# Output projections of both layers from seven half-size products, PSUM banks of the first pinned, one embedding product moved ahead of the turned rows

## Time and profile before

| | |
|---|---|
| median of 3 runs | 1343.76 us (1342.78 to 1344.82) |
| the profiled execution's own time | 1345.24 us |
| its span, first to last instruction | 1343.3 us |
| TensorE busy (matmul) | 1058.4 us, 79% |
| VectorE / ScalarE / GpSimd busy | 412.1 / 179.7 / 90.7 us |
| mean granted TensorE clock | 0.918 of full speed |
| moved by DMA | 474.88 MB, mean 354 GB/s |

### The profile page before, as it was taken

How to read it: one execution, slowest core, us unless ns; L and a number is a source line. 1 busy time by engine, 2 the same in 40 slices (tenths; PEclk the granted TensorE clock), 3 DMA queues, 4 the chain that set the end, 5 groups by cost and what they waited for, 6 DMA issues and landing times.

```text
span 1343.3 us, 26339 instructions
## 1 busy us (share of the span) xinstructions
PE 1058.4 (79%) x10962; PEld 628.8 (47%) x10962; DVE 412.1 (31%) x884; ACT 179.7 (13%) x429; POOL 90.7 (7%) x227
## 2 busy tenths in 40 slices
PE   6999988666677667679999999988666765776578
PEld 5885444333344334344688554445333433433343
DVE  1694323112112111226674544432111111121116
ACT  2344311000000000011121000221000000000001
POOL 0100011000000000000110100011000000000000
PEclk9999999888888888899999999999888888888889
DMA  9846799999999999999454236699999999999992
GB/s 360 322 162 245 293 406 427 428 428 428 428 428 428 429 429 429 428 414 367 153 188 148 103 126 239 279 395 426 428 428 429 429 428 428 428 427 429 429 421 100
DMA packets 57841, 474.88 MB, mean 354 GB/s; under 512 B 4057, under 2 KB 6105, under 8 KB 32193
## 3 DMA queue, kind: packets, MB, share of 16 engines
q1 hardware_dynamic: 56800, 470.32, 84.9%
q10 hardware_dynamic: 768, 2.57, 0.5%
q0 software_dynamic: 224, 1.31, 0.3%
HBM read 473.12 MB, written 3.16 MB: 355 GB/s over the span
## 4 chain that ended last, share of the span: by engine, by line
DMA 49%; PE 45%; DVE 2%; issue 2%; ACT 1%; SPq 1%; POOL 0%; DVEq 0%; ACTq 0%; POOLq 0%
DMA big<-in_moe_w_up_dram 48%; PE ps L920 10%; PE ps L663 7%; PE ps L1105 5%; PE ps L686 4%; PE ps L1019 3%; PE ps L654 3%; PE ps L733 2%; PE ps L644 2%; PE ps L1167 2%; PE ps L942 1%; PE ps L831 1%; PE ps L950 1%; SPq L527 1%; PE ps L848 1%
## 5 line engine op out<-in xcount | busy, mean ns | idle before, releaser
L920 PE MATMUL ps<-big 128*32 128x256 f32 x4064 | 322.6, 485 | 161.2 <-DMA big<-in_moe_w_up_dram 161.0
L920 PEld LDWEIGHTS ps<-big 128*32 128x32 f32 x4064 | 166.1, 138 | 312.5 <-issue 179.7
L1741 DVE SCALAR_TENSOR_TENSOR big<-big,ps 64x256 f32<-64x256 f32 x64 | 26.4, 413 | 684.0 <-ACT big L1361 684.0
L942 PE MATMUL ps<-big 128*32 128x256 f32 x2048 | 123.8, 382 | 57.5 <-DVE big L1750 57.5
L942 PEld LDWEIGHTS ps<-big 128*32 128x32 f32 x2048 | 59.9, 109 | 107.6 <-DVE big L1750 74.4
L950 PE MATMUL ps<-big 32*128 32x256 f32 x1024 | 73.3, 398 | 41.9 <-ACT big L1372 40.6
L1361 ACT ACTIVATE big<-ps 64x256 f32<-64x256 f32 x64 | 24.2, 378 | 568.6 <-PE ps L920 568.6
L663 PE MATMUL ps<-big,xT 128*128 128x512 f32 x224 | 98.2, 593 | 1.3 <-ACT xT L1214 1.3
L950 PEld LDWEIGHTS ps<-big 32*128 32x128 f32 x1024 | 49.5, 184 | 70.8 <-issue 70.8
L2164 POOL TENSOR_TENSOR big<-big,rk 128x64 f32<-128x64 f32 x64 | 19.0, 296 | 775.0 <-PE ps L929 745.4
L890 PE MATMUL ps<-xn,big 128*32 128x256 f32 x1056 | 69.3, 379 | 0.0
(11 more groups left out here) (251 smaller groups left out, 1011.3 us busy)
## 6 DMA issues: line engine op xcount, KB each, us to landing
big<-in_moe_w_gate_dram SPq DMA_DIRECT2D x64, 2048.0 KB, 33.1
big<-in_moe_w_down_dram SPq DMA_DIRECT2D x62, 2048.0 KB, 38.7
big<-in_moe_w_up_dram SPq DMA_DIRECT2D x60, 2048.0 KB, 37.3
big<-in_od_w_in_dram SPq DMA_DIRECT2D x12, 2048.0 KB, 13.0
big<-in_ev_w_in_dram SPq DMA_DIRECT2D x6, 2048.0 KB, 20.7
big<-in_ple_w_gate_dram SPq DMA_DIRECT2D x8, 1024.0 KB, 19.1
big<-in_od_w_out_dram SPq DMA_DIRECT2D x4, 2048.0 KB, 7.8
big<-in_moe_w_up_dram SPq DMA_DIRECT2D x6, 1024.0 KB, 35.4
```

Source lines behind the costliest of these rows:

```text
L920: ins = nc.tensor.matmul(ps[TOK * i:TOK * i + TOK, 5, 0:2 * P].rearrange("p (b n) -> p b n", b=2), xe[:, k, :], (low if k < KD // 2 else w ...
L942: ins = nc.tensor.matmul(ps[TOK * q:TOK * q + TOK, 7, 0:QD], hidT[:, k, :], wd[:, k, q * QD:(q + 1) * QD], start=k == 0, stop=k == KF - 1)
```

## The change

- Layer 0's projection: for either block (now called pair 0 and 1) `out_product` does seven products of 2 matmuls each in place of 16 matmuls; the second pair adds onto the banks of the first (no fresh start). VectorE makes three weight tiles (128 x 1024) and four token sums (128 x 256) per pair ahead, a fourth tile later, and recombines the parts into `h`; ScalarE copies one bank out.
- Layer 1's projection: blocks `rout0` and `rout1` become a pair too, 7 x 4 matmuls; products a and a2 stand at step 10, the other five after `gain_rows(1)`; then the second pair as before, onto the same banks. On VectorE the first tile of pair 0 is made at the end of step 8, its sums and tiles (`out_parts(0)`) at step 10, `gain_diagonals(1)` directly after the loop, and the sums and tiles of pair 1 after that.
- The jobs of layer 0's projection and `gain0` get fixed banks. Before, these five jobs took five turns of the rotating counter; now they take none.
- `embed(0, 0, 0)`, one matmul, is moved ahead of `turn_rows(0)` in both layers.
- Loads: slot 0 and slot 1 in layer 1, and slots 0 and 7 in layer 0, are reloaded once all products of pair 0 have been done; the spare load of layer 0 now follows expert 2's loads.

The diff, cut to its core:

```diff
-LAST_BANKS = {"last_b": "yT3_0", "last_d": "yT3_1", "last_c": "gain1"}
+LAST_BANKS = {"rout_01": "yT3_0", "rout_10": "yT3_1"}
...
-    moe = lambda l: ([f"ffnT{l}_00", f"ffnT{l}_01", f"up{l}_00", f"route{l}_0", f"ffnT{l}_10", f"ffnT{l}_11", f"up{l}_01",
+    moe = lambda l: ([f"up{l}_00", f"ffnT{l}_00", f"ffnT{l}_01", f"route{l}_0", f"ffnT{l}_10", f"ffnT{l}_11", f"up{l}_01",
...
-    jobs += [f"out_{t}{n}" for t in range(2) for n in range(2)] + ["gain0"]
+    jobs += [f"out_{i}" for i in ("a", "00", "b", "d", "c", "01", "10")] + ["gain0"]
...
     jobs += [f"rq0T_{t}" for t in range(NT)]
...
-    rout = [f"rout_{t}{n}" for t in range(2) for n in range(2)]
     for i in range(HEAD_STEPS):
-        jobs += rout if i == HEAD_STEPS - 2 else []
+        jobs += ["last_a", "rout_00"] if i == HEAD_STEPS - 2 else []
...
-    jobs += ["gain1"] + [f"last_{i}" for i in "abdc"]
+    jobs += ["gain1"] + [f"last_{i}" for i in "bdc"] + ["rout_01", "rout_10"]
...
         fixed |= {f"acc{l}_{q}": q for q in range(QUARTERS)}
+        fixed |= {f"out_{i}": b for b, i in enumerate(("00", "d", "10", "gain", "a", "01", "c", "b")) if i != "gain"}
+        fixed["gain0"] = 3
...
                         elif i == RING + 1 and l == 0:
-                            sync.wait_ge(block_read, BLOCK_READ["out0"])
-                            sync.dma_start(held(SPARE, KD, BLK), eg[l][:, AHEAD[1], :, :]).then_inc(spare_landed, 16)
+                            sync.wait_ge(out_read, len(OUT_READS))
                         elif i == RING + 1:
-                            sync.wait_ge(out_tiles_ready, 4)
...
                         expert(l, kind, e, e)
+                full(sync, ("out_c", "rout_10")[l])
                 if l:
-                    full(sync, "rout_10")
                     sync.wait_ge(out_parts_used, 1)
-                    sync.dma_start(held(SPARE, KD, BLK), eg[l][:, AHEAD[1], :, :]).then_inc(spare_landed, 16)
+                sync.dma_start(held(SPARE, KD, BLK), eg[l][:, AHEAD[1], :, :]).then_inc(spare_landed, 16)
...
+            def out_product(l, pair, i):
+
+                B11, T1, B21, B22 = out_quarters(l, pair)
...
+                lhs, rhs = {"a": (A11, B11), "a2": (A12, B21), "b": (S1, T1), "d": (S2, T2), "c": (S3, T3), "b2": (S4, B22),
+                            "c2": (A22, T1)}[i]
+                sums, tiles = {"a": (0, 0), "a2": (0, 0), "b": (1, 1), "d": (2, 2), "c": (3, 3), "b2": (4, 0), "c2": (4, 4)}[i]
+                if sums:
+                    pe.wait_ge(out_sums_ready, 4 * (2 * l + pair) + sums)
+                if tiles:
+                    pe.wait_ge(out_tiles_ready, OUT_TILES[l][pair][tiles - 1])
+                job = OUT_JOBS[l][i]
+                if pair == 0:
+                    out_banks[job] = begin(job)
+                half = HALF if l else HALF // 2
+                for k in range(half):
+                    ins = nc.tensor.matmul(out_banks[job], lhs[:, k, :], rhs[:, k, :], start=k == 0 and pair == 0,
+                                           stop=k == half - 1 and pair == 1, skip_group_check=True)
+                if pair == 1:
+                    end(job, ins)
+                elif i in OUT_READS:
+                    ins.then_inc(out_read, 1)
...
-            outs = held_rows("out")
-            outs(lambda k, t: gaT[:, k, t * P:(t + 1) * P], "out0", 0, 8)
+            arrived("out0")
+            for i in ("a", "a2", *OUT_READS):
+                out_product(0, 0, i)
             gain_rows(0)
...
-            outs(lambda k, t: ybT[:, k - 4, t * P:(t + 1) * P], "out1", 4, 8)
+            for i in ("a", "b", "d", "a2", "b2", "c", "c2"):
+                out_product(0, 1, i)
...
+                embed(0, 0, 0)
                 turn_rows(0)
-                for k in range(2):
-                    embed(0, 0, k)
+                embed(0, 0, 1)
...
+
+                for c in range(2):
+                    arrived(f"rout{c}")
+                    for t in range(NT):
+                        taken(pe, f"yT{c}_{t}")
+                out_product(1, 0, "a")
+                out_product(1, 0, "a2")
...
                 if hd == HEAD_STEPS - NT:
-                    out_block(0)
+                    out_begun()
...
-            out_block(1)
             gain_rows(1)
+            for i in OUT_READS:
+                out_product(1, 0, i)
...
+            for i in ("a", "b", "d", "c", "a2", "b2", "c2"):
+                out_product(1, 1, i)
...
                 copy_out(f"pv{c}", ybT[:, 2 * c:2 * c + 2, :].rearrange("p m s -> p (m s)"), bank(f"pv{c}"))
+
+            copy_out("out_a", first_part, bank("out_a"))
...
+                out, left, right = ((T1, T1, B11), (T2, B22, T1), (T3, T2, B11), (T1, B21, T2))[n]
+                if n:
+                    dve.wait_ge(out_tiles_ready, OUT_TILES[l][pair][min(n, 2) - 1])
+                ve.tensor_tensor(out, left, right, ALU.subtract).then_inc(out_tiles_ready, 1)
...
+                out, left, right = ((S1, A21, A22), (S2, S1, A11), (S3, A11, A21), (S4, A12, S2))[n]
+                if n % 2:
+                    dve.wait_ge(out_sums_ready, 4 * (2 * l + pair) + (1 if n == 1 else 2))
+                ve.tensor_tensor(out, left, right, ALU.subtract if n else ALU.add).then_inc(out_sums_ready, 1)
...
-            gain_diagonals(0)
-            add_rows("out", 1)
+            out_arrived("out0", "out1")
+            for pair in range(2):
+                for n in range(3):
+                    out_tile(0, pair, n)
+                    if pair == 0:
+                        out_sum(0, 0, n)
+                if pair == 0:
+                    out_sum(0, 0, 3)
+                    gain_diagonals(0)
+            for c in range(2):
+                taken(dve, f"pv{c}")
+            for n in range(4):
+                out_sum(0, 1, n)
+            out_read_by(0, "b")
+            out_tile(0, 0, 3)
+            gain_turned(0)
...
+            for job, part in (("out_00", h11), ("out_01", h12)):
+                full(dve, job)
+                emptied(job, ve.tensor_tensor(part, part, bank(job), ALU.add))
+                taken(dve, job)
+            dve.sem_inc(h_ready, 1)
+            full(dve, "out_c")
+            v(ve.tensor_tensor(h21, h21, bank("out_c"), ALU.add))
+            emptied("out_c", ve.tensor_tensor(h22, h22, bank("out_c"), ALU.add))
+            normalise(1, 0)
+            v.sync()
+            full(dve, "out_10")
+            emptied("out_10", ve.tensor_tensor(h21, h21, bank("out_10"), ALU.add))
+            taken(dve, "out_c")
+            taken(dve, "out_10")
+            dve.sem_inc(h_ready, 1)
...
-            B11, B12, B21, B22 = out_quarters()
+            def out_parts(pair):
+
+                if pair:
+                    out_read_by(1, "b")
+                out_sum(1, pair, 0)
+                if pair:
+                    out_read_by(1, "d")
+                out_sum(1, pair, 1)
+                out_tile(1, pair, 1)
+                if pair:
+                    out_read_by(1, "c")
+                out_sum(1, pair, 2)
+                out_tile(1, pair, 2)
+                if pair:
+                    out_read_by(1, "b2")
+                out_sum(1, pair, 3)
...
+                    out_arrived("rout0", "rout1")
+                    out_tile(1, 0, 0)
                 if hd == NH + GATE_LAG:
...
-                        dve.wait_ge(landed[loads.at[f"rout{c}"]], 16 * loads.turn[f"rout{c}"])
...
+            gain_diagonals(1)
+            gain_turned(1)
+            out_read_by(1, "b")
+            out_tile(1, 0, 3)
+            out_arrived("rout2", "rout3")
+            out_tile(1, 1, 0)
             for c in (2, 3):
...
+            out_parts(1)
...
             full(dve, "last_b")
-            ve.tensor_tensor(B12, B21, OT2, ALU.subtract).then_inc(out_tiles_ready, 1)
+            out_tile(1, 1, 3)
```

More of the change, by code:

```diff
@@ L110 @@
 SEVEN = ("rk0", "rk1", "rv0", "rv1", "rv2", "rv3")
-LAST_BANKS = {"last_b": "yT3_0", "last_d": "yT3_1", "last_c": "gain1"}
+LAST_BANKS = {"rout_01": "yT3_0", "rout_10": "yT3_1"}
+OUT_READS = "b", "d", "c", "b2", "c2"
+OUT_JOBS = [{i: f"{w}_{i}" for i in "abcd"} | {f"{i}2": f"{r}_{n}" for i, n in (("a", "00"), ("b", "01"), ("c", "10"))}
+            for w, r in (("out", "out"), ("last", "rout"))]
+OUT_TILES = ((1, 2, 3, 7), (4, 5, 6, 8)), ((9, 10, 11, 12), (13, 14, 15, 16))
 GATE_LAG, BACK_LAG = 2, 4
@@ L297, in trunk, with out_quarters @@
         rkraw = view(5120 + NH * VD + BLK, NT, 512)
[L298 to L303, removed]
+        def out_quarters(l, pair):
+            k = HALF if l else HALF // 2
+            if l:
+                blocks = [held(loads.at[f"rout{2 * pair + i}"], HALF, D) for i in range(2)]
+            else:
+                blocks = [slot(f"out{pair}", HALF, D)[:, k * i:k * i + k] for i in range(2)]
+            return [w[:, :, BLK * j:BLK * j + BLK] for w in blocks for j in range(2)]
+        out_sums = [[[view(SLOT + S * i, 2, P) for i in range(4)], [view(D + S * i, 2, P, base=xT2) for i in range(4)]],
```

(37 more changed lines are left out.)

56 lines of the change are left out of this document (29 added, 27 removed).

## The result

Median of 4 runs after: 1354.66 us (1352.72 to 1358.40); of 4 runs before: 1343.87 us (1342.78 to 1344.82). The ratio is 1.0083, 95% interval [1.0071, 1.0096]: slower by 10.8 us. The execution that was profiled is the slowest of the four, 1358.4 us with a span of 1356.6, against 1345.24 and 1343.3 before.

What follows compares the result with a forecast made beforehand. Expert stages were taken as fixed DMA transfer behind a start TensorE sets. -2.35 + 6.9 + 0.65 + 4.6 = +9.8 us, against the median of 1343.76, gave 1353.6; range 1347.5 to 1357.5.

Steps and rivals of the forecast that it cites:

- The clock's 4.6 us: TensorE's granted clock falls behind the new waits of 3.85 and 4.4 us in layer 1, 2.3 us each: +4.6 us.
- Products: -3.44 us per layer: TensorE in both layers' projections: four program matmuls fewer per layer at 0.86 us each, 6.9 us less in all.
- the turned rows, where I had 0.3: Layer 1's projection: turned rows no longer wait for `rout_10`, but `route(0)` waits for ScalarE; 0.3 us won.
- Layer 0: -2.35: Layer 0's projection: its experts start 2.35 us earlier, of 3.44 saved, with VectorE's norm and last add on the path.
- Start of layer 1: +6.9: Start of layer 1: `rq` jobs move from banks 0 to 3 to banks 3 to 6 and wait: +6.9 us.
- 0.85 for `rq0_0`: Start of layer 1: `rq0_0`, in bank 3, waits for VectorE's read of `gate0_c2`: 0.85 us.
- 2.2 for `mixT1_11`: Start of layer 1: `mixT1_11`, in bank 3, waits for `rq0_0`'s rotation, delaying `rq0_1` by 2.2 us more.
- 3.85 for `rk0_a`: Start of layer 1: `rk0_a`, in bank 4, waits for VectorE's rotation of `rq1_0`: 3.85 us of TensorE.
- Layer 1's projection: +0.65: Layer 1's projection: 4.4 us lost before the gain, 3.44 won on products, 0.3 on turned rows: +0.65 us.
- where I had 4.4: Layer 1's projection: TensorE waits at `gain_rows(1)` for VectorE's diagonals, from 817.2 to 821.6: 4.4 us lost.
- the rival of a third fall: Start of layer 1: the clock also falls in two short waits around `mixT1_11`, another 2.3 us, 1355.9; chance 0.15.
- The embedding product and the loads: The moved embedding product only fills the wait for the turned rows, and the loads keep up: no cost.

Runs made afterwards that it cites:

- Experiment 3: Kernel after the change, with layer 1's banks as before (counter moved on five at `gain0`) and its gain diagonals ahead of the sums: 1339.65 us, ratio 0.9970.
- experiment 6: Kernel after the change, with matmuls whose results nothing reads put into TensorE's waits at layer 1's start and before its gain rows: 1349.25 us, ratio 1.0045.
- experiment 1: Kernel after the change, with the bank counter moved on by five at `gain0`, giving layer 1's first products their old banks: 1345.36 us, ratio 1.0013.
- experiment 5: Kernel before the change, with only its bank counter set back by five at `gain0`: 1356.00 us, ratio 1.0087.
- experiment 7: Kernel after the change, with the bank counter moved on by two at `gain0`: 1348.24 us, ratio 1.0027.
- Experiment 2: Kernel after the change, with layer 1's gain diagonals built ahead of the sums on VectorE: 1348.54 us, ratio 1.0035.
- Experiment 4: Kernel of experiment 3, with the first embedding product put back behind the turned rows in both layers: 1338.23 us, ratio 0.9956.

## Why the prediction was right, point by point

1354.66 us stands against a forecast of 1353.6. The sign, the three places and their waits were right. The clock's 4.6 us agree with the medians, but one place where it fell was missed.

- **Products: -3.44 us per layer.** Experiment 3 has -3.81 us from the first product of `rout` to `route(0)`. The products themselves, first start to last end, take 856.64 - 806.76 = 49.88 us where they took 862.80 - 809.48 = 53.32: the 3.44. The other 0.37 is for the turned rows, where I had 0.3.
- **Layer 0: -2.35.** Measured -2.55 to `route(0)`. To the first expert only -1.55 was left in the profiled execution, since the clock fell to 0.57 over 4 us there; in experiment 3, where it held, it was -2.56 (165.29 - 122.92 = 42.37, before 44.93). I had given this place no fall.
- **Start of layer 1: +6.9.** Measured 7.41 with the clock held (experiment 6). The three terms: 0.85 for `rq0_0` was an idle of 0.87, the first matmul coming 1.04 later counted from the turned rows; 2.2 for `mixT1_11` was 2.33 (from `rq0_0` to `rq0_1` 18.38 us, before 16.05); 3.85 for `rk0_a` was a wait of 3.86, and 3.92 from start to start with the clock held (experiment 6: `rq0_1` to `rk0_a` 18.60 us, before 14.68). Experiments 1, 5 and 7 show that the cause of these waits is the bank's last holder.
- **Layer 1's projection: +0.65.** Measured +0.33 (experiment 6). The wait was 4.15 where I had 4.4: this is the term that was sized too high. Experiment 2 shows that VectorE's order makes it.
- **The clock: +4.6 for two falls.** Both came: 1.7 and 2.4 us by their windows, 4.1 together. The step that failed is the rival of a third fall. I gave it 0.15, since 2.22 us of waiting had left the clock alone; it came in all three traces that have these waits unfilled, those of the kernel after (2.8 us) and of experiments 2 (16.85 us of products in place of 13.97) and 5 (1.7 us). One row of a wait with busy work around it was too little to exclude a fall behind two waits in a row. The Trainium skill, "TensorE: Matmul & The Clock Gate", section "A second HAM failure mode: psum-queue depth-cycling", describes frequent short idles between matmul groups as enough to make the clock swing; the traces agree, with waits of 2.04 and 1.28 us.
- **What the clock costs by the medians.** Experiment 6 gives 5.4 us; experiment 3 gives 15.0 - 7.41 - 4.14 = 3.5, its gain less the waits (4.14 is 53.07 against 57.21 from `rout` to `route(0)`). My 4.6 lie between the two, so the runs do not show that the term was too low as a sum, though it left out one place. All three falls together, 6.9 us, are seen only in the profiled execution of the kernel after, its slowest.
- **The stages against the medians.** In experiment 6, where the clock held, -2.56 + 7.41 + 0.33 = 5.2 us by stage stand against 5.1 by the medians. In experiment 3 the stages give -2.56 - 3.81 = -6.4 us and the medians -4.3. The sum of the terms above can so be checked against a median to some 2 us only, and that 1354.66 came within 1.1 us of 1353.6 is in part luck.
- **The embedding product and the loads** were costed at nothing. Experiment 4 shows it for the first. For the loads, both expert stages take what they took (458.75 us after and 459.03 before to the turned rows of layer 1, 464.22 and 463.75 to the end), with the DMA share as full as before.

What isn't settled: why the clock fell behind `route(0)` in the traces of the kernel after and of experiment 2 and not in those of 1, 3, 6 and 7, which have the same waits there; and why experiment 3's median gains 2 us less than its stages do. Nor was it tried which of the filling matmuls of experiment 6 are needed.

## What to carry to other kernels

When buffers are handed out by a counter, adding or pinning one job moves all that come after it, far from the edit: write out who held each buffer before, for the old and the new order, and price the late ones. The Trainium skill, "Perfetto Trace Analysis", section "Matmuls", advises to rotate independent groups through the PSUM banks; here all variants rotate, and by whose bank they met the same groups cost 0 (experiment 3), 4.2 (experiment 7) or 11.9 us more (the kernel after). Price a wait of TensorE twice, once as idle time and once as the slower matmuls that may stand behind it: in the traces here 1.7 us (behind 2.03 us of waiting, experiment 7) to 3.0 us (behind 4.16 us, also there, with 0.50 over the next 6 us), and nothing behind one of 2.22 us. And put small work that another engine waits for ahead of the large work on its own engine.

## What the runs showed of the hardware that I had not expected

- The granted clock fell behind a wait of only 2.03 us (0.72 over the next 6 us, experiment 7), though 2.22 us had left it at 1.00. The length of one wait alone doesn't decide.
- It can fall within a wait: over the 4.15 us before the gain of layer 1 it was already 0.76 on the mean, while over the 3.85 us before `rk0_a` it was 1.00. The same wait before the gain has 0.90 in experiment 7, so its length doesn't set this.
- In layer 0 no single wait ahead of the fall was longer than 0.95 us, and executions with the same order of work there had it or not: the windows 151 to 153 and 153 to 155 us have 0.73 and 0.50 in experiment 2, 1.00 and 1.00 in experiment 1.
- Matmuls without use, put into the waits, made the kernel 5.4 us faster.
- Layer 0's first product started between 120.60 and 122.92 us in the nine traces, though TensorE's work ahead of it is the same in all: 2.3 us of spread between executions are there before any of this begins.
